# Small gate rows turned by plain transposes and added by VectorE, with the gathers of the next experts moved into the large blocks

## The chip, the core and the metric

The kernel runs on one core of one Trainium2 chip. The metric is device time in microseconds (us) of one execution.

## The reference: what is computed

One sequence of 256 tokens (two tiles of 128), model width 1024, float32. Layer 0 is retention and a dense SwiGLU; layer 1 is attention and a mixture of 8 experts, of which each token uses two. A layer norm follows each of the four parts. The change touches only the experts:

```
def swiglu(x, w_in, w_out):
    gate, up = jnp.split(x @ w_in, 2, axis=-1)
    return (jax.nn.silu(gate) * up) @ w_out

def moe_swiglu(x, router, w_in, w_out):
    ...
    for e in range(N_EXPERTS):
        out = out + gates[:, e:e + 1].astype(x.dtype) * swiglu(xt, w_in[e], w_out[e])
```

Each expert has a hidden width of 3584, so its weights are 1024 x 7168 and 3584 x 1024.

## The kernel before, in words

**Weights in units.** All weights stream through SBUF in units of 1 MB (128 x 2048 floats). SyncE issues one transfer for each unit into a ring of eight raw buffers (raw, more_raw). ScalarE copies the unit to its rounded high part (whi, whi_more), VectorE subtracts to get the low part (wlo, wlo_more), and TensorE multiplies with both. In the expert stage there are four such pairs, so ScalarE may split unit n + 4 only when TensorE is done with unit n (semaphore unit_used), and SyncE may refill a raw buffer only when VectorE is done with it (lo_done).

**Jobs.** The eight experts are sorted by how many tokens they have. They are worked in four pairs of a large job (up to 128 tokens) and a small job (up to 64 tokens); jobs 0, 2, 4, 6 are large and 1, 3, 5, 7 small. In a large job every weight unit takes 12 matmuls of 512 columns: x_hi with whi, x_hi with wlo, x_lo with whi. In a small job the 64 high and the 64 low token rows lie side by side in one 128-row operand, so that a unit takes 8 matmuls (with whi and with wlo). Rows 0 to 63 of the product then hold the part of the high rows, rows 64 to 127 that of the low rows, and the two have to be added.

**Blocks.** The hidden width of an expert is cut into blocks 0 to 3, of 1024, 1024, 1024 and 512 columns. A block has four gate units and four up units (two and two in block 3), and its output units follow a block later. The table STREAM lists all 336 units in the order of work: block b of the large job (gate units, output units of the block before, up units), then block b of the small job, then block b + 1 of the large job, and so on. Here such a piece of 8, 10 or 12 units is called a large stretch or a small stretch. START is the number of the first unit of a stretch, END that of the last unit of one part.

**Order on the engines.** Every engine runs the same loop over the unit number n, in its own queue. Tables such as GATE_TURN_AT say at which n it also does a piece of the work between. TensorE at n: unit n, then turns, then gathers. ScalarE at n: row copies, the high part of unit n + 4, then the small drains, then the copies of a gather. VectorE at n: the drains, then the low part of unit n + 4. So what VectorE does at n stands ahead of the low part of unit n + 4.

**The gate of a small block.** At END of the gate units ScalarE copies the two banks of gate rows to rows4. Two units later TensorE turns them by matmuls against the table merge (two identities of 64 one above the other, so that the product is transposed and the low row is added to the high row at once): turn_merged, 8 chunks (4 in block 3) into bank 0. Then ScalarE takes the silu into act_small. The up rows go the same way, and VectorE multiplies the two.

**Gathers.** The token rows of the next pair of jobs are gathered by matmuls with a selection matrix in 8 steps of 4 matmuls of 192 columns (gather_step), into bank 1; ScalarE copies each out (L956, L957). Before, three steps are in block 1 of the large job, three in block 1 of the small job and two in block 2 of the large job, for each of three pairs.

Of the kernel before, what the change touches and what calls it, by code (L numbers as in the profile page):

```python
# [6 lines left out]
ALU = mybir.AluOpType  # L7
# [7 lines left out]
P = 128  # L15
# [14 lines left out]
def build(nc, x, ln_g, ln_b, ret_w_in, ret_gn_g, ret_gn_b, ret_w_out, kv_w, moba_w_q, moba_w_out,  # L30
# [29 lines left out]
    JOBS = EX  # L60
# [26 lines left out]
    for phase in range(JOBS * (LAST + 1)):  # L87
# [5 lines left out]
        else:  # L93
# [12 lines left out]
    GATE_AT = {END[j, "gate", b]: (j, b) for j, b in SMALL_BLOCKS}  # L106
    GATE_TURN_AT = {END[j, "gate", b] + 2: (j, b) for j, b in SMALL_BLOCKS}
    UP_AT = {END[j, "up", b]: (j, b) for j, b in SMALL_BLOCKS}
    UP_TURN_AT = {END[j, "up", b] + 1: (j, b) for j, b in SMALL_BLOCKS}
# [4 lines left out]
                 for k, (j, b, i) in enumerate([(2 * pair - 2, 1, 5), (2 * pair - 2, 1, 7), (2 * pair - 2, 1, 9),  # L114
                                                (2 * pair - 1, 1, 5), (2 * pair - 1, 1, 7), (2 * pair - 1, 1, 9),
                                                (2 * pair - 2, 2, 5), (2 * pair - 2, 2, 7)])}
    SEL_AT = {START[j - j % 2, 2] + 1 + 3 * (j % 2): j for j in range(JOBS)}
# [29 lines left out]
    with ctx:  # L147
        def sem(name):
            return ctx.enter_context(nc.semaphore(name))
# [210 lines left out]
        gate_copied = sem("gate_copied")  # L360
        gate_turned = sem("gate_turned")
        small_silu = sem("small_silu")
        up_copied = sem("up_copied")
# [111 lines left out]
        def turn_bank(j, b, half):  # L475

            if j == 0 and b == 0:
                return 4 + half
            return 3 if b == LAST else 2 + half

        def sel_of(j):
# [184 lines left out]
        def _(act):  # L666
# [256 lines left out]
            def small_drains(n):  # L923

                if n in GATE_TURN_AT:
                    j, b = GATE_TURN_AT[n]
                    w = BLOCK_UNITS[b] * P
                    act.wait_ge(gate_turned, blocks(j, b))
                    if blocks(j, b) > 1:
                        act.wait_ge(small_lo, blocks(j, b) - 1)  # L930
                    nc.scalar.activation(act_small[:, 0:w], ps[:, 0, 0:w], ACT.Silu).then_inc(small_silu, 1)
                if n in SMALL_HI_AT:
# [89 lines left out]
        def _(dve):  # L1022
# [391 lines left out]
            def small_drains(n):  # L1414

                if n in SMALL_LO_AT:
                    j, b = SMALL_LO_AT[n]
                    c = 2 * BLOCK_UNITS[b]
                    gT = gT_small_of(j, b)
                    dve.wait_ge(small_hi, blocks(j, b))  # L1420
                    lo_of(gT[:, 0:c, HALF:P], act_small[:, 0:c * HALF].rearrange("p (c n) -> p c n", c=c),
                          gT[:, 0:c, 0:HALF]).then_inc(small_lo, 1)
                if n in SMALL_MUL_AT:
                    j, b = SMALL_MUL_AT[n]
# [76 lines left out]
        def _(pe):  # L1501
# [351 lines left out]
            def gather_pair(n):  # L1853

                pair, k = GATHER_AT[n]
                j, b = 2 * pair - 1 - (k in (0, 1, 2, 6, 7)), 2 if k >= 6 else 1
                if SMALL[j]:
                    pe.wait_ge(gate_copied, halves(j, b))
                else:
                    pe.wait_ge(big_silu, halves(j, b))  # L1860
                if k == 0:
# [48 lines left out]
            def big_unit(n):  # L1910

                j, part, b, q = STREAM[n]
                if q == 0 and part == "gate":
                    if b == 0 and j > 0:
                        pe.wait_ge(big_copied, KD * (j // 2))
                    if blocks(j, b) > 1:
                        pe.wait_ge(small_silu, blocks(j, b) - 1)
                        pe.wait_ge(gate_copied, 7 * (j // 2) + 2 * b)
# [65 lines left out]
            def small_turn(n):  # L1984

                if n in GATE_TURN_AT:
                    j, b = GATE_TURN_AT[n]
                    pe.wait_ge(gate_copied, halves(j, b))
                    turn_merged(rows4, 0, 2 * BLOCK_UNITS[b]).then_inc(gate_turned, 1)
                if n in UP_TURN_AT:  # L1990
# [102 lines left out]
```

## Time and profile before

| | us |
|---|---|
| median of 3 runs | 1430.73 (1428.29 to 1431.02) |
| the profiled execution: its own time | 1427.71 |
| the profiled execution: span of the core's instructions | 1426.0 |
| TensorE, VectorE, ScalarE busy in it | 1392.5, 1132.3, 959.8 |

The profile is that of one execution. Its rows are told in the section after the next. In the names of the rows PE is TensorE, PEld its weight loads, DVE VectorE, ACT ScalarE, SPq the queue of SyncE. A busy TensorE does not mean that it sets the time: its matmuls overlap, and a row's duration is longer than the distance to the next.

### The profile page before, as it was taken

How to read it: one execution, taken by the hardware profiler on the slowest of the kernel's cores; microseconds unless marked ns; L12 is line 12 of the kernel's file. 1: busy time of each engine (PE TensorE's matmuls, PEld its weight loads, DVE VectorE, ACT ScalarE, POOL GpSimd, SP SyncE). 2: the span in 40 equal slices, each digit the busy share in tenths (PEclk: the TensorE clock that was granted, in tenths of full speed). 3: DMA queues.
4: the chain of work that ended last, by engine and by line, in shares of the span. 5: the costliest groups of instructions: out<-in, count | busy, mean ns of one | idle time of the engine just before them, and what ended most of it. 6: DMA issues, size and time to landing. Idle time of an engine off the chain costs nothing.

```text
span 1426.0 us, 18557 instructions
## 1 busy us (share of the span) xinstructions
PE 1392.5 (98%) x7394; PEld 1182.6 (83%) x7394; DVE 1132.3 (79%) x791; ACT 959.8 (67%) x798; POOL 55.2 (4%) x64
## 2 busy tenths in 40 slices
PE   9999999999999999999999999999999999999995
PEld 9987789999979888888788788788788788787784
DVE  4456655454465678998999998999988999999996
ACT  5334544433454458797888797888787887787874
POOL 1002200000000003002000002000000000000000
PEclk9999999999999999999999999999999999999998
DMA  9654546555554329999999999999999999999990
GB/s 358 233 172 151 199 157 213 198 178 178 195 188 155 141 89 387 420 395 405 400 419 420 385 378 418 386 418 420 394 372 419 390 417 420 392 399 421 416 406 32
DMA packets 158743, 446.89 MB, mean 313 GB/s; under 512 B 7088, under 2 KB 46000, under 8 KB 158656
## 3 DMA queue, kind: packets, MB, share of 16 engines
q1 hardware_dynamic: 156832, 439.38, 80.5%
q0 software_dynamic: 1824, 6.33, 1.3%
q8 instruction: 57, 0.93, 0.2%
q14 instruction: 30, 0.25, 0.0%
HBM read 444.63 MB, written 1.05 MB: 313 GB/s over the span
## 4 chain that ended last, share of the span: by engine, by line
PE 68%; DVE 25%; issue 3%; ACT 3%; POOL 0%; DVEq 0%; ACTq 0%; POOLq 0%
PE ps L1504 20%; PE ps L1506 20%; PE ps L1505 20%; DVE wlo L1032 13%; DVE wlo_more L1032 6%; ACT whi L876 2%; PE ps L1980 2%; DVE gT_lo L1032 1%; DVE act L1400 1%; PE ps L1841 1%; DVE h L1391 1%; PE ps L1942 1%; PE ps L1943 1%; PE ps L1550 1%; DVE wlo L418 1%
## 5 line engine op out<-in xcount | busy, mean ns | idle before, releaser
L1032 DVE TENSOR_TENSOR wlo<-raw,whi 128x2048 fp32r<-128x2048 f32 (+1 forms) x214 | 479.1, 2259 | 33.5 <-ACT whi L876 32.8
L876 ACT ACTIVATE whi<-raw 128x2048 fp32r<-128x2048 f32 x208 | 395.7, 1918 | 107.4 <-PE ps L1506 100.7
L418 DVE TENSOR_TENSOR wlo<-raw,whi 128x2048 fp32r<-128x2048 f32 x80 | 183.6, 2294 | 155.3 <-ACT whi L411 155.3
L411 ACT ACTIVATE whi<-raw 128x2048 fp32r<-128x2048 f32 x82 | 156.8, 1912 | 153.2 <-PE ps L1506 149.7
L1504 PE MATMUL ps<-xT_hi,whi 128*128 128x256 f32 x576 | 163.3, 284 | 0.0
L1506 PE MATMUL ps<-xT_hi,wlo 128*128 128x256 f32 x576 | 163.0, 283 | 0.0
L1505 PE MATMUL ps<-xT_lo,whi 128*128 128x256 f32 x576 | 163.0, 283 | 0.0
L1504 PE MATMUL ps<-whi,xg_big 128*128 128x512 f32 x336 | 135.1, 402 | 3.4 <-DVE wlo L1032 3.4
L1942 PE MATMUL ps<-whi,xg_small 128*128 128x512 f32 x336 | 135.0, 402 | 2.7 <-DVE wlo L1032 1.8
L1506 PE MATMUL ps<-whi,xg_big 128*128 128x512 f32 x336 | 132.0, 393 | 0.0
L1505 PE MATMUL ps<-wlo,xg_big 128*128 128x512 f32 x336 | 131.5, 391 | 0.0
L1943 PE MATMUL ps<-wlo,xg_small 128*128 128x512 f32 x336 | 131.4, 391 | 0.0
L1504 PEld LDWEIGHTS ps<-xT_hi,whi 128*128 128x128 f32 x576 | 110.5, 192 | 0.5
L1505 PEld LDWEIGHTS ps<-xT_lo,whi 128*128 128x128 f32 x576 | 110.5, 192 | 0.4
L1506 PEld LDWEIGHTS ps<-xT_hi,wlo 128*128 128x128 f32 x576 | 110.5, 192 | 0.0
L1032 DVE TENSOR_TENSOR wlo<-more_raw,whi 128x2048 fp32r<-128x2048 f32 x42 | 96.1, 2288 | 9.3 <-ACT whi L876 9.3
L1032 DVE TENSOR_TENSOR wlo_more<-more_raw,whi_more 128x2048 fp32r<-128x2048 f32 x42 | 96.1, 2287 | 4.8 <-ACT whi_more L876 4.8
L1032 DVE TENSOR_TENSOR wlo_more<-raw,whi_more 128x2048 fp32r<-128x2048 f32 x42 | 96.1, 2287 | 3.8 <-ACT whi_more L876 3.8
L876 ACT ACTIVATE whi<-more_raw 128x2048 fp32r<-128x2048 f32 x42 | 80.6, 1918 | 18.8 <-PE ps L1506 13.6
L876 ACT ACTIVATE whi_more<-raw 128x2048 fp32r<-128x2048 f32 x42 | 80.6, 1920 | 12.3 <-PE ps L1506 12.3
L876 ACT ACTIVATE whi_more<-more_raw 128x2048 fp32r<-128x2048 f32 x42 | 80.7, 1920 | 12.2 <-PE ps L1506 12.2
L1504 PE MATMUL ps<-whi,xT_hi 128*128 128x512 f32 (+1 forms) x224 | 85.3, 381 | 2.4 <-DVE wlo L418 2.2
(269 smaller groups left out, 2686.5 us busy)
## 6 DMA issues: line engine op xcount, KB each, us to landing
raw<-in_moe_w_in SPq DMA_DIRECT2D x168, 1024.0 KB, 8.6
raw<-in_moe_w_out SPq DMA_DIRECT2D x84, 1024.0 KB, 7.8
more_raw<-in_moe_w_in SPq DMA_DIRECT2D x56, 1024.0 KB, 8.4
more_raw<-in_moe_w_out SPq DMA_DIRECT2D x28, 1024.0 KB, 8.2
raw<-in_ret_w_in SPq DMA_DIRECT2D x23, 1024.0 KB, 7.1
raw<-in_ffn_w_in SPq DMA_DIRECT2D x22, 1024.0 KB, 4.9
raw<-in_ffn_w_out SPq DMA_DIRECT2D x11, 1024.0 KB, 4.9
raw<-in_ret_w_out SPq DMA_DIRECT2D x8, 1024.0 KB, 4.9
```

Source lines behind the costliest of these rows:

```text
L411: nc.scalar.activation(whi[:, u % SPLIT, :], src, ACT.Copy).then_inc(hi_done, 1)
L418: nc.vector.tensor_tensor(wlo[:, u % SPLIT, :], src, whi[:, u % SPLIT, :].bitcast(F32), ALU.subtract).then_inc(lo_done, 1)
L876: nc.scalar.activation(moe_split(n)[0], moe_raw(n), ACT.Copy).then_inc(hi_done, 1)
L1032: return nc.vector.tensor_tensor(dst, src, hi.bitcast(F32), ALU.subtract)
L1391: nc.vector.scalar_tensor_tensor(out=h[:, t, :], in0=ps[:, at:at + 2, :].rearrange("p b n -> p (b n)"), scalar=gate, in1=h[:, t, :], op0=A ...
L1400: nc.vector.tensor_tensor(act4[:, cols], act4[:, cols], ps[:, 2 + half, :], ALU.mult).then_inc(big_mul, 1)
L1504: pe.matmul(dst, a_hi, b_hi, start=start, stop=False, skip_group_check=True)
L1505: pe.matmul(dst, a_hi, b_lo, start=False, stop=False, skip_group_check=True)
L1506: return pe.matmul(dst, a_lo, b_hi, start=False, stop=stop, skip_group_check=True)
L1942: pe.matmul(dst, a, hi, start=start, stop=False, skip_group_check=True)
L1943: return pe.matmul(dst, a, lo, start=False, stop=stop, skip_group_check=True)
L1980: last = pe.matmul(ps[:, at, c * HALF:(c + 1) * HALF], rows[:, c * P:(c + 1) * P], merge[:, :], start=True, stop=True)
```

## The change

Five things are done. The gate rows of a small block are turned by plain transposes against the identity, each of which writes 128 columns, so that the result takes two banks (0 and 1) and the low part is not yet added (turned_gate names the two halves). ScalarE copies the low half to act_small where it took the silu before. VectorE adds the high half at END of gate + 3 (GATE_SUM_AT). ScalarE takes the silu in place at END of gate + 6, or + 4 in the very last small block (SMALL_SILU_AT). And all gathers stand in large blocks: three in block 1, three in block 2 and two in block 3 of the large job. The up rows are still turned against merge.

```diff
--- before.py
+++ after.py
@@ -105,6 +105,8 @@
     LO_AT = {END[j, "up", b] + 3 + half: (j, b, half) for j, b, half in BIG_HALVES}
     GATE_AT = {END[j, "gate", b]: (j, b) for j, b in SMALL_BLOCKS}
     GATE_TURN_AT = {END[j, "gate", b] + 2: (j, b) for j, b in SMALL_BLOCKS}
+    GATE_SUM_AT = {END[j, "gate", b] + 3: (j, b) for j, b in SMALL_BLOCKS}
+    SMALL_SILU_AT = {END[j, "gate", b] + (4 if (j, b) == (JOBS - 1, LAST) else 6): (j, b) for j, b in SMALL_BLOCKS}
     UP_AT = {END[j, "up", b]: (j, b) for j, b in SMALL_BLOCKS}
     UP_TURN_AT = {END[j, "up", b] + 1: (j, b) for j, b in SMALL_BLOCKS}
     SMALL_MUL_AT = {END[j, "up", b] + 2: (j, b) for j, b in SMALL_BLOCKS}
@@ -112,8 +114,8 @@
     SMALL_LO_AT = {END[j, "up", b] + 5: (j, b) for j, b in SMALL_BLOCKS}
     GATHER_AT = {START[j, b] + i: (pair, k) for pair in range(1, JOBS // 2)
                  for k, (j, b, i) in enumerate([(2 * pair - 2, 1, 5), (2 * pair - 2, 1, 7), (2 * pair - 2, 1, 9),
-                                                (2 * pair - 1, 1, 5), (2 * pair - 1, 1, 7), (2 * pair - 1, 1, 9),
-                                                (2 * pair - 2, 2, 5), (2 * pair - 2, 2, 7)])}
+                                                (2 * pair - 2, 2, 5), (2 * pair - 2, 2, 7), (2 * pair - 2, 2, 9),
+                                                (2 * pair - 2, 3, 3), (2 * pair - 2, 3, 5)])}
     SEL_AT = {START[j - j % 2, 2] + 1 + 3 * (j % 2): j for j in range(JOBS)}
     Y_AT = {END[j, "out", LAST]: j for j in range(JOBS - 1)}
     SCATTER_AT = {END[j, "out", LAST] + (4 + 4 * t if j < JOBS - 2 else 3 + 3 * t): (j, t) for j in range(JOBS - 1) for t in range(T)}
@@ -359,6 +361,8 @@
         big_lo = sem("big_lo")
         gate_copied = sem("gate_copied")
         gate_turned = sem("gate_turned")
+        gate_half = sem("gate_half")
+        gate_summed = sem("gate_summed")
         small_silu = sem("small_silu")
         up_copied = sem("up_copied")
         up_turned = sem("up_turned")
@@ -477,6 +481,9 @@
             if j == 0 and b == 0:
                 return 4 + half
             return 3 if b == LAST else 2 + half
+
+        def turned_gate():
+            return ps[:, 0:2, :].rearrange("p a (c s n) -> p (a c) s n", s=2, n=HALF)
 
         def sel_of(j):
             return sel[:, j // 2 % 2, :, j % 2 * P:(j % 2 + 1) * P]
@@ -924,11 +931,17 @@
 
                 if n in GATE_TURN_AT:
                     j, b = GATE_TURN_AT[n]
-                    w = BLOCK_UNITS[b] * P
+                    c = 2 * BLOCK_UNITS[b]
                     act.wait_ge(gate_turned, blocks(j, b))
                     if blocks(j, b) > 1:
                         act.wait_ge(small_lo, blocks(j, b) - 1)
-                    nc.scalar.activation(act_small[:, 0:w], ps[:, 0, 0:w], ACT.Silu).then_inc(small_silu, 1)
+                    nc.scalar.activation(act_small[:, 0:c * HALF].rearrange("p (c n) -> p c n", c=c),
+                                         turned_gate()[:, 0:c, 1, :], ACT.Copy).then_inc(gate_half, 1)
+                if n in SMALL_SILU_AT:
+                    j, b = SMALL_SILU_AT[n]
+                    w = BLOCK_UNITS[b] * P
+                    act.wait_ge(gate_summed, blocks(j, b))
+                    nc.scalar.activation(act_small[:, 0:w], act_small[:, 0:w], ACT.Silu).then_inc(small_silu, 1)
                 if n in SMALL_HI_AT:
                     j, b = SMALL_HI_AT[n]
                     c = 2 * BLOCK_UNITS[b]
@@ -1420,6 +1433,12 @@
                     dve.wait_ge(small_hi, blocks(j, b))
                     lo_of(gT[:, 0:c, HALF:P], act_small[:, 0:c * HALF].rearrange("p (c n) -> p c n", c=c),
                           gT[:, 0:c, 0:HALF]).then_inc(small_lo, 1)
+                if n in GATE_SUM_AT:
+                    j, b = GATE_SUM_AT[n]
+                    c = 2 * BLOCK_UNITS[b]
+                    rows = act_small[:, 0:c * HALF].rearrange("p (c n) -> p c n", c=c)
+                    dve.wait_ge(gate_half, blocks(j, b))
+                    nc.vector.tensor_tensor(rows, rows, turned_gate()[:, 0:c, 0, :], ALU.add).then_inc(gate_summed, 1)
                 if n in SMALL_MUL_AT:
                     j, b = SMALL_MUL_AT[n]
                     w = BLOCK_UNITS[b] * P
@@ -1853,11 +1872,7 @@
             def gather_pair(n):
 
                 pair, k = GATHER_AT[n]
-                j, b = 2 * pair - 1 - (k in (0, 1, 2, 6, 7)), 2 if k >= 6 else 1
-                if SMALL[j]:
-                    pe.wait_ge(gate_copied, halves(j, b))
-                else:
-                    pe.wait_ge(big_silu, halves(j, b))
+                pe.wait_ge(big_silu, halves(2 * pair - 2, 1 + k // 3))
                 if k == 0:
                     pe.wait_ge(sel_ready, 2 * T * pair)
                 pe.wait_ge(small_copied, gathers(pair) + k)
@@ -1914,7 +1929,7 @@
                     if b == 0 and j > 0:
                         pe.wait_ge(big_copied, KD * (j // 2))
                     if blocks(j, b) > 1:
-                        pe.wait_ge(small_silu, blocks(j, b) - 1)
+                        pe.wait_ge(gate_summed, blocks(j, b) - 1)
                         pe.wait_ge(gate_copied, 7 * (j // 2) + 2 * b)
                     if gathered_by(START[j, b]):
                         pe.wait_ge(small_copied, gathered_by(START[j, b]))
@@ -1986,7 +2001,9 @@
                 if n in GATE_TURN_AT:
                     j, b = GATE_TURN_AT[n]
                     pe.wait_ge(gate_copied, halves(j, b))
-                    turn_merged(rows4, 0, 2 * BLOCK_UNITS[b]).then_inc(gate_turned, 1)
+                    for c in range(2 * BLOCK_UNITS[b]):
+                        last = pe.transpose(ps[:, c // 4, c % 4 * P:(c % 4 + 1) * P], rows4[:, c * P:(c + 1) * P], ident[:, :])
+                    last.then_inc(gate_turned, 1)
                 if n in UP_TURN_AT:
                     j, b = UP_TURN_AT[n]
                     pe.wait_ge(up_copied, halves(j, b))
```

The lists below are the order of instructions on an engine, before and after. A line number of after.py is not that of before.py: L1032 became L1045 (the low part), L1428 became L1447 (multiply by up), L876 became L883 (the high part), L1841 became L1860 (gather).

**VectorE, small stretch of block 1 of job 3, before**, from the second drain of the large job (gT_lo) to the end of the stretch's splits:

```order
L1032 TENSOR_TENSOR gT_lo<-ps,gT_hi 128x512 [waits big_hi]
L1032 TENSOR_TENSOR wlo_more<-more_raw,whi_more 128x2048 [waits hi_done]
L1032 TENSOR_TENSOR wlo<-raw,whi 128x2048 [waits hi_done] x3
L1032 TENSOR_TENSOR wlo_more<-raw,whi_more 128x2048 [waits hi_done]
L1032 TENSOR_TENSOR wlo<-raw,whi 128x2048 [waits hi_done] x2
```

The same place after:

```order
L1045 TENSOR_TENSOR gT_lo<-ps,gT_hi 128x512 [waits big_hi]
L1045 TENSOR_TENSOR wlo_more<-more_raw,whi_more 128x2048 [waits hi_done]
L1045 TENSOR_TENSOR wlo<-raw,whi 128x2048 [waits hi_done] x2
L1441 TENSOR_TENSOR act_small<-act_small,ps 128x512 [waits gate_half]
L1045 TENSOR_TENSOR wlo<-raw,whi 128x2048 [waits hi_done]
L1045 TENSOR_TENSOR wlo_more<-raw,whi_more 128x2048 [waits hi_done]
L1045 TENSOR_TENSOR wlo<-raw,whi 128x2048 [waits hi_done] x2
```

The sum (L1441) stands three splits ahead of the end; the first of the last two wlo rows is the first unit of the next large stretch, so the sum stands ahead of that.

**TensorE, large stretch of block 3 of job 0**, from the fourth unit (its output products, gT_hi) into the fifth, before:

```order
L1504 MATMUL ps<-whi_more,gT_hi 128x512
L1505 MATMUL ps<-wlo_more,gT_hi 128x512
L1506 MATMUL ps<-whi_more,gT_lo 128x512
L1504 MATMUL ps<-whi,gT_hi 128x512
L1505 MATMUL ps<-wlo,gT_hi 128x512
```

and after:

```order
L1524 MATMUL ps<-wlo_more,gT_hi 128x512
L1525 MATMUL ps<-whi_more,gT_lo 128x512
L1860 MATMUL ps<-sel,h_hi 128x192 x2
L1860 MATMUL ps<-sel,h_lo 128x192 x2
L1523 MATMUL ps<-whi,gT_hi 128x512
```

A gather step has come in between the two units. The same happens two units later, and once more in block 2.

**ScalarE, the very last small block (job 7, block 3)**, from its up rows (L907) on, before:

```order
L907 ACTIVATE rows_116<-ps 128x512
L876 ACTIVATE whi_more<-raw 128x2048
L931 ACTIVATE act_small<-ps 128x256
L876 ACTIVATE whi<-raw 128x2048 x2
L963 ACTIVATE y_hi_106<-ps 128x512 x2
L876 ACTIVATE whi<-more_raw 128x2048
```

and after:

```order
L914 ACTIVATE rows_116<-ps 128x512
L883 ACTIVATE whi_more<-raw 128x2048
L938 ACTIVATE act_small<-ps 128x256
L883 ACTIVATE whi<-raw 128x2048 x2
L944 ACTIVATE act_small<-act_small 128x256
L976 ACTIVATE y_hi_106<-ps 128x512 x2
L883 ACTIVATE whi<-more_raw 128x2048
```

The silu (L944) now stands behind the two splits that it stood ahead of (as L931), and VectorE's multiply in that block stands ahead of the low part of the second of these two units.

## Rows read from the trace of the kernel before

**Rows 1.** The page: busy time by engine; the chain that ended last, by engine.

```profile
PE 1392.5 (98%) x7394; PEld 1182.6 (83%) x7394; DVE 1132.3 (79%) x791; ACT 959.8 (67%) x798; POOL 55.2 (4%) x64
...
PE 68%; DVE 25%; issue 3%; ACT 3%; POOL 0%; DVEq 0%; ACTq 0%; POOLq 0%
```

**Rows 2.** Waits, 540 to 1402 us: who waited for whom, us, times, longest.

```profile
ACT whi L876 <- PE ps L1506: 113.6, 119, 3.5
...
PE ps L1504 <- DVE wlo L1032: 3.4, 14, 0.5
```

**Rows 3.** SyncE's own queue, 600 to 1400 us, the same columns.

```profile
SPq L544 <- DVE wlo L1032: 471.4, 225, 3.5
```

**Rows 4.** Chain in order of time, 820 to 960 us: start, us, what.

```profile
826.09 1.93 ACT whi L876
...
843.73 6.60 DVE wlo L1032 x3
...
852.54 2.21 DVE wlo L1032
854.88 0.47 PE ps L1504
...
857.89 1.73 PE ps L1980 x16
...
873.84 0.42 PE ps L1841 x4
...
955.31 2.22 DVE wlo L1032
957.66 0.47 PE ps L1504
```

**Rows 5.** The same view, 735 to 800 us.

```profile
791.58 0.47 PE ps L1504
```

**Rows 6.** Busy time by stretch: TensorE, weight loads, VectorE, ScalarE, GpSimd; clock, DMA share, GB/s.

```profile
828.00:854.80 26.80, 26.70 (x136) 22.10 (x134) 26.77 (x16) 25.72 (x25) 0.00 (x0) 1.00 1.01 380
854.90:890.00 35.10, 35.10 (x168) 29.37 (x169) 30.48 (x15) 26.08 (x23) 7.96 (x4) 1.00 1.02 418
```

**Rows 7.** VectorE's groups by shape, 540 to 1402 us: busy us, mean ns.

```profile
L1428 DVE TENSOR_TENSOR act_small<-act_small,ps 128x512 f32<-128x512 f32 x12 | 8.2, 682 | 0.0
L1428 DVE TENSOR_TENSOR act_small<-act_small,ps 128x256 f32<-128x256 f32 x4 | 1.7, 413 | 0.0
```

**Rows 8.** VectorE in order of time, from 830 us: start, us, what.

```profile
830.24 0.68 DVE L1400 TENSOR_TENSOR act<-act,ps 128x512 f32<-128x512 f32 x1
830.84 2.28 DVE L1032 TENSOR_TENSOR wlo_more<-raw,whi_more 128x2048 fp32r<-128x2048 f32 x1
```

**Rows 9.** ScalarE in order of time, 837 to 850 us.

```profile
843.38 0.61 ACT L931 ACTIVATE act_small<-ps 128x512 f32<-128x512 f32 x1
```

**Rows 10.** TensorE in order of time, from 612.4 us, and from 1411 us.

```profile
612.40 0.39 PE L1943 MATMUL ps<-wlo,xg_small 128*128 128x512 f32 x1
612.63 0.60 PE L1906 MATMUL ps<-ident,act 128*128 128x128 f32 x4
612.98 0.48 PE L1942 MATMUL ps<-whi,xg_small 128*128 128x512 f32 x1
...
1412.88 0.63 PE L1877 MATMUL ps<-y_lo_last,selT 128*128 128x512 f32 x1
1413.31 0.63 PE L1876 MATMUL ps<-y_hi_last,selT 128*128 128x512 f32 x1
```

**Rows 11.** VectorE, then ScalarE, in order of time, end of the expert stage.

```profile
1392.76 2.29 DVE L1032 TENSOR_TENSOR wlo<-raw,whi 128x2048 fp32r<-128x2048 f32 x1 [0.73 <-ACT whi L876]
1394.96 0.41 DVE L1428 TENSOR_TENSOR act_small<-act_small,ps 128x256 f32<-128x256 f32 x1
1396.42 2.30 DVE L1032 TENSOR_TENSOR wlo<-raw,whi 128x2048 fp32r<-128x2048 f32 x1 [1.04 <-ACT whi L876]
...
1394.47 1.92 ACT L876 ACTIVATE whi<-raw 128x2048 fp32r<-128x2048 f32 x1 [1.75 <-PE ps L1506]
```

## The prediction

> **What bounds the kernel now.** I read the page first. TensorE is busy for 98% of the span and VectorE for 79%, which would make TensorE the bound everywhere; but the chain that ended last gives TensorE 68% and VectorE 25% [rows 1]. A quarter of the time is therefore set by VectorE. The question is where.
>
> The chain in order of time answers it. At 826.09 it passes from TensorE to a split on ScalarE (whi), and from there to VectorE. From then until 854.88 it holds only VectorE pieces: three low parts in a row from 843.73, and the last one at 852.54, which is the first unit of the next large stretch. At 854.88 it goes back to TensorE, at the first matmul of that unit [rows 4]. The same handing over stands at 957.66, after the low part at 955.31 [rows 4], and at 791.58 [rows 5]. So a large stretch is set by TensorE (12 matmuls for each unit), and a small one (8 matmuls for each unit) by VectorE, whose low part costs 2.20 us of chain whatever the job. The stretches show it too: between 828.00 and 854.80 VectorE is busy for 26.77 of 26.80 us, and between 854.90 and 890.00 for only 30.48 of 35.10 [rows 6].
>
> The waits agree. TensorE's first matmul of a large unit (L1504) waits for VectorE's low part 14 times, 3.4 us in all [rows 2]: short, but it means that at the end of the small stretches TensorE had already caught up with VectorE. In the other direction ScalarE waits 119 times for TensorE (L1506, large units) [rows 2], which is how a large stretch holds back the splits. Do the transfers bind? SyncE's queue waits 471.4 us for VectorE to give a buffer back [rows 3], and no wait of an engine for a landing stands among the waits that I read. They do not.
>
> **The change, part by part.** The price of each edit hangs on whether it stands in a large stretch (TensorE sets the end) or in a small one (VectorE does).
>
> *Fewer passes on TensorE.* A merge matmul runs as two passes: 8 chunks are x16 in the chain and take 1.73 us [rows 4], 0.108 a pass. Four plain transposes start at 612.63 and the next matmul at 612.98; that one takes 0.48 us where its like take 0.39, so four cost some 0.43, or 0.108 each [rows 10]. A chunk so falls from 0.216 to 0.108 us. There are 12 wide small blocks of 8 chunks and 4 narrow ones of 4, 112 chunks in all: TensorE is given 12.1 us less to do. All of it lies in small stretches, under VectorE's work, and there TensorE is the one that waits. I take it as nothing. Its bounds are 0 and -12.1.
>
> *The sum on VectorE.* It is a tensor_tensor from act_small and PSUM, the form of L1428: 0.682 us for 512 columns, 0.413 for 256 [rows 7]. Consecutive instructions overlap: one of 0.68 us starts at 830.24 and the next at 830.84 [rows 8], so in a full queue a wide sum costs 0.60 and, with the same overlap of 0.08, a narrow one 0.33. It stands ahead of the low part of unit END of gate + 7. In blocks 1 and 2 this is two units ahead of the next large stretch, in blocks 0 and 3 the first unit of that stretch. Either way it is ahead of the low part for which TensorE waits. Two blocks differ. In job 1, block 0, where no output units stand between gate and up, the sum comes behind the low part of the large stretch's second unit, and the large stretch covers it. In job 7, block 3, it falls into a gap of 0.73 us ahead of 1392.76 [rows 11]. That leaves 11 wide and 3 narrow ones on the path: 11 x 0.60 + 3 x 0.33 = 7.6 us.
>
> Does VectorE also wait there? The sum needs ScalarE's copy, and that stands where the silu stood: 843.38, for 0.61 us [rows 9]. The sum's place is between the second and the third of the low parts that run from 843.73 [rows 4], at 848.1. ScalarE is over 4 us early, so I take no wait. The copy of the low half reads as many columns as the silu did, so I price it the same. The sum reads PSUM in runs of 64 columns, which no VectorE row here shows; from below I price it at the 0.60 above, from above at double, 7.6 us more.
>
> *The silu on its own.* ScalarE gets one more activation for each small block, at most 0.61 us [rows 9]. ScalarE is busy for 25.72 of the 26.80 us of a small stretch [rows 6], which is close, but three pairs of gather copies leave that stretch, and the silu comes four units after the old one, when VectorE's multiply is still four units away. I take it as nothing, except at the end.
>
> *The end.* In job 7, block 3, the silu stands behind the high part of unit 333, which starts at 1394.47 and takes 1.92 us; VectorE's multiply stands ahead of the low part of unit 333. Now that multiply runs at 1394.96, in a gap, and the low part starts at 1396.42 as soon as the high part is there [rows 11]. After the change the order is high part (to 1396.4), silu (0.3), multiply (0.33), low part: it starts at about 1397.1, 0.7 us late. From there VectorE's work is in one piece into the last output units. +0.7 us; at worst +1.0.
>
> *The gathers.* A step of four matmuls takes 0.42 us of chain [rows 4]. Three for each of three pairs leave a small stretch, where TensorE gains nothing by it, and enter large stretches, where TensorE sets the time: +1 in block 2 and +2 in block 3. I looked at whether they still stand ahead of the place where the chain leaves TensorE. In block 2 that is ten units in, and the last gather follows the unit before; in block 3 it is six units in, and the gathers follow units three and five. So 9 x 0.42 = 3.8 us; the lower bound is 0, if VectorE had lain ahead there. The ScalarE copies go into the 2.7 us (12 x 0.23 [rows 10]) for each unit of a large stretch, where ScalarE is busy for 26.08 of 35.10 us [rows 6].
>
> *Waits.* TensorE's next gate units now wait for the sum (gate_summed) and no longer for the silu. Behind that wait stand the matmuls of the whole large stretch; but they wait for a later low part of the same queue anyway, so it is never the last to come.
>
> Sum: 7.6 + 0.7 + 3.8 = +12.1 us. The profiled execution's own time is 1427.71, of which 1426.0 is the span: that gives 1439.8 and 1438.1. The median before is 3.0 us above that execution, so against it the same change gives 1442.8; I say 1442.5.
>
> **The rivals.**
>
> *Faster: the saving on TensorE counts.* If TensorE set the small stretches too, the change would take away up to 12.1 us there and the sums would be covered. With the gathers only moved from one bound place to another, the time would be about 1419. For it: 98% busy. Against it: the chain and the 14 waits. It decides at the handing over: where TensorE reaches the large stretch's first unit later than its low part, the saving counts, and there only until the 0.60 us sum has used it up. 4%.
>
> *No change: the transfers set the pace.* The DMA share is 1.01 in the small stretch [rows 6], so a memory-bound stage would hide the sums, the gathers and the saving alike: 1431. The chain has no transfer in it, and SyncE waits for VectorE, not VectorE for a landing. 3%. The Trainium skill (Perfetto Trace Analysis, Roofline) says that a single core can be taken to have its ceiling at about 120% of 358 GB/s, bounded by 16 DMA engines of some 435 GB/s together; by that rule the 418 GB/s of a large stretch is nearly full and no VectorE term would count. The waits in this trace speak against it.
>
> *Dearer sums.* The short PSUM runs or a wait make each sum cost up to double, or the sums shift a second thing late: 1447 to 1451. 7%.
>
> *Cheaper.* The gathers or some of the sums find cover: 1434 to 1438. 7%.
>
> *The clock.* TensorE waits longer at the end of each small stretch (some 2 to 3 us more, what it saves plus the sum), right behind a burst of transposes. If the granted clock fell there to the lower level, the matmuls would be 0.43 us apart, as at the end of this trace (1412.88 to 1413.31) [rows 10], in place of 0.23 (612.40 to 612.63): a large unit would take 2.4 us longer, and one such unit in each of 14 stretches 34 us, or 1477. Against it: a clock of 1.00 in both stretches, with four transposes twice in each small one [rows 6]. 2%. The Trainium skill (TensorE: Matmul & The Clock Gate, Part 4: PE-mode transpose) says that transposes do not count as busy for the clock, and 8 in a row would by it be a risk that merge was not.
>
> **How the numbers follow.** My forecast, 1439.5 to 1446 by itself, has 77%. The range takes in the cheaper case from 1437 and the dearer one to 1449. A measurement here tells 0.2% (2.9 us) from no change; everything from 1434 up is slower. So slower 0.92, within 0.2% 0.04, faster 0.04.
>
> **What would show it.** Right: L1441 x16 on VectorE at about 0.68 and 0.41 us and in the chain 14 times; the small stretches of blocks 1 to 3 longer by one sum; waits of TensorE for VectorE's low part up from a few us to 25 or so, since TensorE arrives early; gathers in the chain nine times more; transposes x112 where 224 merge passes were. Wrong: a chain without L1441, VectorE idle ahead of it, or a clock under 1.00 in a small stretch.

## The result and the profile after

| | before | after |
|---|---|---|
| median (range) | 1430.34 us (1428.29 to 1431.02), 4 runs | 1446.57 us (1446.14 to 1450.81), 4 runs |
| ratio, 95% interval | | 1.0125 (1.011 to 1.014) |
| profiled execution, its span | 1427.71, 1426.0 us | 1446.54, 1444.8 us |

The change makes the kernel 1.25% slower. The medians are 16.2 us apart, the two profiled spans 18.8 us. Lines have moved: the low part is now L1045, the high part L883, a large unit's matmuls L1523 to L1525, a small unit's L1957 and L1958, the merge L1995, a gather step L1860, VectorE's multiply L1447. New are L1441 (the sum), L944 (the silu by itself) and L2005 (the plain turns).

The page after: busy time, then the share of each engine in the chain that ended last.

```profile
PE 1391.5 (96%) x7282; PEld 1171.3 (81%) x7282; DVE 1141.0 (79%) x807; ACT 967.2 (67%) x814; POOL 54.9 (4%) x64
PE 66%; DVE 27%; issue 4%; ACT 3%; POOL 0%; DVEq 0%; ACTq 0%; POOLq 0%
```

Against [rows 1] the span has grown by 18.8 us and TensorE's busy time has not: it gained idle time. Between 600 and 1400 us it was idle for 7.8 us before (busy 792.19 of 800) and is idle for 22.2 us after (busy 777.77). VectorE has 16 instructions more, and a larger share of the chain. Where TensorE's idle time is, the waits after between 540 and 1421 say (total us, times, longest):

```profile
PEld ps L1957 <- DVE wlo L1045: 18.7, 22, 1.7
PEld ps L1957 <- DVE wlo_more L1045: 15.5, 23, 0.9
PE ps L1957 <- DVE wlo L1045: 10.7, 19, 1.3
PE ps L1523 <- DVE wlo L1045: 6.1, 14, 1.1
DVE act_small L1447 <- ACT act_small L944: 4.5, 2, 2.8
PEld ps L1523 <- DVE act_small L1441: 3.3, 1, 3.3
```

The first two are waits of the weight loads of a small stretch for the low parts, with their matmuls' own waits in the third; in the same view of before the first two were this:

```profile
PEld ps L1942 <- DVE wlo L1032: 7.8, 13, 1.0
PEld ps L1942 <- DVE wlo_more L1032: 5.7, 15, 0.5
```

The handing over to a large stretch (fourth row) is still there 14 times, and has grown from 3.4 us [rows 2] to 6.1. TensorE works faster through a small stretch and then waits longer for VectorE. The last row is new and was not forecast: one single wait of 3.3 us for the sum.

The chain after, around the same stretches as [rows 4]:

```profile
852.17 2.20 DVE wlo_more L1045
854.37 4.41 DVE wlo L1045 x2
858.78 0.60 DVE act_small L1441
859.37 2.20 DVE wlo L1045
...
866.13 0.47 PE ps L1523
...
869.13 1.73 PE ps L1995 x16
...
885.12 0.42 PE ps L1860 x4
...
891.01 0.42 PE ps L1860 x4
...
896.91 0.42 PE ps L1860 x4
```

The sum stands in the chain for 0.60 us, between two low parts with no gap, and the three gathers of block 2 stand in the part where the chain is on TensorE. Between 560 and 1421 the chain has 15 such pieces of L1441: 12 of 0.59 to 0.61 and 3 of 0.33 us. A gather step stands in it 24 times (21 of 0.42 and 3 of 0.52 us), against 15 before (12 and 3): nine more, as forecast. VectorE's groups by form and TensorE's turns (busy us, mean ns):

```profile
L1441 DVE TENSOR_TENSOR act_small<-act_small,ps 128x512 f32<-128x512 f32 x12 | 8.2, 683 | 0.0
L1441 DVE TENSOR_TENSOR act_small<-act_small,ps 128x256 f32<-128x256 f32 x4 | 1.7, 415 | 0.0
```

```profile
L2005 PE MATMUL ps<-ident,rows 128*128 128x128 f32 x112 | 14.8, 272 | 0.0
```

The sum costs what the multiply costs [rows 7], although it reads PSUM in runs of 64 columns.

**Where the 18.8 us lie.** Stages can be cut where VectorE starts the low part of a given unit. Unit 0 is the first of the experts, unit 16 the first of the large stretch that follows the first small one, unit 28 the first of the next small stretch, unit 324 the first of the last small stretch. Two of these marks in the timeline of VectorE, of before and then of after (start, duration, instruction):

```profile
602.59 2.29 DVE L1032 TENSOR_TENSOR wlo<-raw,whi 128x2048 fp32r<-128x2048 f32 x1 [0.89 <-ACT whi L876]
1372.11 2.29 DVE L1032 TENSOR_TENSOR wlo<-raw,whi 128x2048 fp32r<-128x2048 f32 x1
```

```profile
609.76 2.29 DVE L1045 TENSOR_TENSOR wlo<-raw,whi 128x2048 fp32r<-128x2048 f32 x1 [0.88 <-ACT whi L883]
1390.67 2.28 DVE L1045 TENSOR_TENSOR wlo<-raw,whi 128x2048 fp32r<-128x2048 f32 x1
```

All kernels of this study, cut the same way (the rows above are units 28 and 324):

| kernel | start of unit 0 | 0 to 16 | 16 to 28 | 28 to 324 | 324 to end |
|---|---|---|---|---|---|
| before | 524.1 | 46.4 | 32.1 | 769.5 | 53.8 |
| after | 526.9 | 46.4 | 36.4 | 780.9 | 54.1 |
| e1_first_sum_early | 527.1 | 50.8 | 32.6 | 780.9 | 53.6 |
| e2_gathers_only | 524.0 | 46.4 | 32.1 | 773.4 | 53.0 |
| e3_vector_op_only | 524.0 | 46.4 | 32.1 | 777.1 | 52.9 |
| e4_turns_no_sum | 527.3 | 46.4 | 32.1 | 773.5 | 52.9 |
| e7_wait_only | 524.0 | 46.4 | 36.4 | 769.4 | 52.9 |
| e6_gathers_small | 526.8 | 46.4 | 32.1 | 766.4 | 53.0 |
| e5_up_rows_instead | 527.1 | 50.7 | 31.2 | 758.4 | 53.1 |
| e8_up_rows_gathers_small | 524.9 | 46.4 | 31.1 | 755.7 | 52.2 |

Each row is one execution. Where nothing was edited and the clock is alike, the stages agree within 0.1 us: 46.4, 32.1, and 769.5 in before with 769.4 in e7.

So 18.8 = 2.8 ahead of the experts + 4.3 in the first large stretch after a small one + 11.4 in the long middle + 0.3 at the end. The 2.8 us are not counted as the change's: no edit touches that code, and the granted clock between 200 and 300 is 0.98 in this execution and 1.00 in that of before. e6, which is made from the kernel before, has them too (526.8). e4, made from the changed kernel, has them in its profiled execution (1434.07 us), and others of its runs took 3.4 us less (1430.71). The two parts to explain are the 11.4 and the 4.3; the 0.3 at the end hides a term of the change and is taken up with the prediction.

### The profile page after: what moved, and what is told of

It is laid out like the page before. It is cut to its first block, busy times and chain, and to the rows that moved or that the text cites. A ratio compares the mean times of both kernels' runs of the same rounds, so it can differ in the third digit from the quotient of the medians.

```text
span 1444.8 us, 18365 instructions
## 1 busy us (share of the span) xinstructions
PE 1391.5 (96%) x7282; PEld 1171.3 (81%) x7282; DVE 1141.0 (79%) x807; ACT 967.2 (67%) x814; POOL 54.9 (4%) x64
## 4 chain that ended last, share of the span: by engine, by line
PE 66%; DVE 27%; issue 4%; ACT 3%; POOL 0%; DVEq 0%; ACTq 0%; POOLq 0%
PE ps L1523 20%; PE ps L1525 20%; PE ps L1524 20%; DVE wlo L1045 14%; DVE wlo_more L1045 6%; ACT whi L883 2%; PE ps L1995 2%; PE ps L1860 1%; DVE gT_lo L1045 1%; DVE act L1413 1%; DVE h L1404 1%; DVE wlo L422 1%; PE ps L1569 1%; DVE act_small L1441 1%; DVE h L1088 1%
## 5 line engine op out<-in xcount | busy, mean ns | idle before, releaser
L1045 DVE TENSOR_TENSOR wlo<-raw,whi 128x2048 fp32r<-128x2048 f32 (+1 forms) x214 | 479.8, 2261 | 36.5 <-ACT whi L883 35.9
L883 ACT ACTIVATE whi<-raw 128x2048 fp32r<-128x2048 f32 x208 | 396.1, 1920 | 113.6 <-PE ps L1525 105.8
L1523 PE MATMUL ps<-xT_hi,whi 128*128 128x256 f32 x576 | 163.7, 284 | 0.0
L1525 PE MATMUL ps<-xT_hi,wlo 128*128 128x256 f32 x576 | 163.3, 284 | 0.0
L1957 PE MATMUL ps<-whi,xg_small 128*128 128x512 f32 x336 | 136.5, 406 | 11.0 <-DVE wlo L1045 10.7
L1523 PE MATMUL ps<-whi,xg_big 128*128 128x512 f32 x336 | 136.3, 406 | 8.9 <-DVE wlo L1045 6.1
L1525 PE MATMUL ps<-whi,xg_big 128*128 128x512 f32 x336 | 132.4, 394 | 0.0
L1958 PE MATMUL ps<-wlo,xg_small 128*128 128x512 f32 x336 | 131.7, 392 | 0.0
L1523 PEld LDWEIGHTS ps<-xT_hi,whi 128*128 128x128 f32 x576 | 110.7, 192 | 0.5
L1525 PEld LDWEIGHTS ps<-xT_hi,wlo 128*128 128x128 f32 x576 | 110.6, 192 | 0.0
L1045 DVE TENSOR_TENSOR wlo<-more_raw,whi 128x2048 fp32r<-128x2048 f32 x42 | 96.1, 2289 | 9.8 <-ACT whi L883 9.8
L1045 DVE TENSOR_TENSOR wlo_more<-more_raw,whi_more 128x2048 fp32r<-128x2048 f32 x42 | 96.1, 2288 | 4.4 <-ACT whi_more L883 4.4
L1045 DVE TENSOR_TENSOR wlo_more<-raw,whi_more 128x2048 fp32r<-128x2048 f32 x42 | 96.1, 2288 | 3.8 <-ACT whi_more L883 3.8
L883 ACT ACTIVATE whi<-more_raw 128x2048 fp32r<-128x2048 f32 x42 | 80.7, 1920 | 18.2 <-PE ps L1525 12.9
L1957 PEld LDWEIGHTS ps<-whi,xg_small 128*128 128x128 f32 x336 | 63.1, 188 | 36.1 <-DVE wlo L1045 18.7
L883 ACT ACTIVATE whi_more<-raw 128x2048 fp32r<-128x2048 f32 x42 | 80.7, 1922 | 13.3 <-PE ps L1525 12.5
L883 ACT ACTIVATE whi_more<-more_raw 128x2048 fp32r<-128x2048 f32 x42 | 80.7, 1921 | 13.1 <-PE ps L1525 12.2
```

The source lines that it names most:

```text
L883: nc.scalar.activation(moe_split(n)[0], moe_raw(n), ACT.Copy).then_inc(hi_done, 1)
L1045: return nc.vector.tensor_tensor(dst, src, hi.bitcast(F32), ALU.subtract)
L1523: pe.matmul(dst, a_hi, b_hi, start=start, stop=False, skip_group_check=True)
L1525: return pe.matmul(dst, a_lo, b_hi, start=False, stop=stop, skip_group_check=True)
L1957: pe.matmul(dst, a, hi, start=start, stop=False, skip_group_check=True)
L1958: return pe.matmul(dst, a, lo, start=False, stop=stop, skip_group_check=True)
```

## The experiments

Eight kernels, in two sessions. Each session ran the kernel before as well: 1428.84 us in the first (e1 to e4), 1429.14 in the second. Every ratio is to the kernel before of the same session. Theory A is that of the prediction: VectorE's sums and TensorE's gathers are added, TensorE's saving is not. The rest was open: the 4.3 us. Of each edit the lines that matter are shown; ... marks a cut inside a piece, and lines that go with them (new semaphores, the wait ahead of a gather step) are left out.

### e1_first_sum_early: the first sum one unit earlier

After, with this:

```
-    GATE_SUM_AT = {END[j, "gate", b] + 3: (j, b) for j, b in SMALL_BLOCKS}
+    GATE_SUM_AT = {END[j, "gate", b] + (2 if (j, b) == (1, 0) else 3): (j, b) for j, b in SMALL_BLOCKS}
```

> The changed kernel, with the one sum of job 1, block 0, placed one unit earlier in VectorE's queue, ahead of the low part of unit 17. Theory (a wait that I left out): TensorE waits at unit 16 for that sum, 2.89 us, and the clock falls behind it; so the wait shrinks to about 0.5 us, the clock stays at 1.00 there, and the time is about 4 us below the changed kernel's 1446.6, near 1442.5, that is 12 above before. Rival (the 4 us came with the run, not with the wait): the time stays within 1.5 us of 1446.6 and the clock dips at the same place.

Measured: 1442.28 us (1439.46 to 1446.82), ratio to before 1.0079 (1.0055 to 1.0103). The stretch 16 to 28 falls from 36.4 to 32.6 us. The wait between 560 and 640, and the window 560 to 580 (busy us of PE, PEld, DVE, ACT, POOL, then the granted clock):

```profile
PEld ps L1523 <- DVE act_small L1441: 1.1, 1, 1.1
```

```profile
560.00:580.00 20.00, 19.48 (x94) 15.71 (x92) 17.66 (x11) 18.80 (x14) 0.00 (x0) 1.00 1.03 421
```

The wait falls from 3.3 to 1.1 us, the clock stays at 1.00, and 3.8 of the 4.3 us are gone. The other 0.5 us is the sum's own, which the chain of e1 still holds (580.24, 0.61 us): the first matmul of unit 16 starts 2.94 us after the start of that unit's low part (580.89 and 577.95), against 2.43 in the kernel before (572.92 and 570.49). The span of the profiled execution, 1445.1, does not show the gain, since in it the clock was 0.83 between 520 and 560, where 0 to 16 took 50.8 us in place of 46.4. That is ahead of the place of the edit, and e5 shows the same. The medians agree in sign and are less exact: 13.4 us over before in e1, 16.2 after the change.

### e2_gathers_only: before, with the gathers moved

```
-                                                (2 * pair - 1, 1, 5), (2 * pair - 1, 1, 7), (2 * pair - 1, 1, 9),
-                                                (2 * pair - 2, 2, 5), (2 * pair - 2, 2, 7)])}
+                                                (2 * pair - 2, 2, 5), (2 * pair - 2, 2, 7), (2 * pair - 2, 2, 9),
+                                                (2 * pair - 2, 3, 3), (2 * pair - 2, 3, 5)])}
```

> The kernel before, with only the gathers moved into the large blocks. Theory (large stretches are set by TensorE, small ones by VectorE): 9 steps of 0.42 us enter the path and nothing leaves it, +3.8 us. Rival (the small stretches are set by TensorE too, or the gathers are covered in the large ones): within 1 us of before.

Measured: 1433.52 us (1430.53 to 1439.03), ratio 1.0035 (1.0017 to 1.0052). The middle grows from 769.5 to 773.4, by 3.9 us; the forecast term was 3.8.

### e3_vector_op_only: before, with one more VectorE instruction

Before, and VectorE takes the maximum of act_small with itself (the same value) in 15 small blocks, where the sum stands after the change; the merge stays.

```
+                if n in GATE_SUM_AT:
+                    ...
+                    nc.vector.tensor_tensor(act_small[:, 0:w], act_small[:, 0:w], act_small[:, 0:w],
+                                            ALU.max).then_inc(gate_summed, 1)
```

> The kernel before, with one more VectorE operation in every small block but the first, at the place of the sum: the maximum of act_small with itself (512 or 256 columns, the result unchanged). Theory: VectorE sets the small stretches, so 11 wide ones at 0.60 and 3 narrow ones at 0.33 us cost 7.6 us. Rival (TensorE or the transfers set them): under 1 us. If the sum of the changed kernel is dearer than this for its way of reading PSUM, this run shows less per operation than the changed kernel does.

Measured: 1435.56 us (1434.31 to 1446.14), ratio 1.0057 (1.0037 to 1.0077). The middle is 777.1 us, 7.6 more than before: 11 wide at 0.60 and 3 narrow at 0.33.

### e4_turns_no_sum: after, without the sum

The silu reads the turned high rows straight from PSUM; the low part of the small gate rows is left out of the result, so that nothing is added on VectorE. The separate silu and the sum are gone, and TensorE waits for the silu again in place of the sum. The gathers and the plain transposes are as after.

```
-                                         turned_gate()[:, 0:c, 1, :], ACT.Copy).then_inc(gate_half, 1)
+                                         turned_gate()[:, 0:c, 0, :], ACT.Silu).then_inc(small_silu, 1)
```

> The changed kernel without the sum: the silu is taken straight from the high half, where the copy was, and the low part of the small gate rows is left out. It has the plain transposes and the moved gathers. Theory: the 12 us that TensorE is given less to do are worth nothing, so it costs what the gathers alone cost, +3.8 us over before. Rival (the saving on TensorE counts): up to 12 us below that, some 8 us faster than before.

Measured: 1432.25 us (1430.71 to 1442.05), ratio 1.0024 (1.0005 to 1.0044). The middle is 773.5 us, the same as e2's 773.4: 112 plain transposes in place of 224 merge passes are worth nothing there. What TensorE is given back turns into waiting, as the waits between 600 and 1400 show; both groups are larger than those of before:

```profile
PEld ps L1946 <- DVE wlo_more L1040: 14.5, 22, 0.9
PEld ps L1946 <- DVE wlo L1040: 13.8, 22, 1.7
```

### e7_wait_only: before, with the first block's wait alone

e3's instruction in job 1, block 0 only, and TensorE waits for it where it waits for the sum of that block after the change:

```
+                        pe.wait_ge(gate_summed, 1)
```

> The kernel before, with one VectorE operation more, in job 1, block 0 alone, at the place where the changed kernel has its sum, and with TensorE's next gate units waiting for it. Theory (a wait that I left out): TensorE waits for it at unit 16, about 2.9 us, the clock falls for a few us behind that wait, and the first large stretch grows by about 4.3 us; all else as before, so +4. Rival (the rest of the change brought those 4 us): no more than 0.6 us.

Measured: 1433.7 us (1430.93 to 1442.67), ratio 1.0031 (1.0013 to 1.0048). The stretch 16 to 28 takes 36.4 us, exactly as after; the other stages are those of before, or of e2 and e3 where these did not touch them. TensorE's timeline, of before at the first matmul of unit 16 and then of e7:

```profile
572.92 0.47 PE L1504 MATMUL ps<-whi,xg_big 128*128 128x512 f32 x1
```

```profile
572.42 0.39 PE L1953 MATMUL ps<-wlo_more,xg_small 128*128 128x512 f32 x1
575.60 0.51 PE L1513 MATMUL ps<-whi,xg_big 128*128 128x512 f32 x1 [2.79 <-DVE act_small L1429]
575.90 0.63 PE L1514 MATMUL ps<-wlo,xg_big 128*128 128x512 f32 x1
576.33 0.63 PE L1515 MATMUL ps<-whi,xg_big 128*128 128x512 f32 x1
...
579.32 0.40 PE L1513 MATMUL ps<-whi,xg_big 128*128 128x512 f32 x1
579.55 0.39 PE L1514 MATMUL ps<-wlo,xg_big 128*128 128x512 f32 x1
```

One wait for one short instruction, without a transpose or a gather moved, gives the whole 4.3 us. Unit 16 starts 2.7 us later than before (575.60 against 572.92; unit 0 starts at 524.0 and 524.1). The other 1.6 us come behind the start, where the matmuls are 0.43 us apart (575.90, 576.33) up to 579.32, where they are 0.23 apart again: 3.7 us hold some nine of them, 0.20 us further apart each, which by this estimate makes 1.7 us.

### e6_gathers_small: the gathers the other way

Before, with the two steps per pair that stood in block 2 of the large job put into block 2 of the small job.

```
-                                                (2 * pair - 2, 2, 5), (2 * pair - 2, 2, 7)])}
+                                                (2 * pair - 1, 2, 5), (2 * pair - 1, 2, 7)])}
```

> The kernel before, with the two gather steps of each pair that stood in block 2 of the large job moved to block 2 of the small job: the opposite of the change. Theory: TensorE waits there for VectorE about 0.85 us in each stretch, room for two steps of 0.42, and 6 steps leave the large stretches: up to 2.5 us faster. Rival (no room, the steps cost the same there): no change.

Measured: 1425.81 us (1423.46 to 1431.98), ratio 0.9973 (0.9956 to 0.9989). The middle falls by 3.1 us; the chain has 9 gather steps in place of 15, and six of 0.42 are 2.5. Where the other 0.6 us comes from was not traced.

### e5_up_rows_instead: the same trade in the other kind of stretch

Gate rows as before; now it is the up rows (in all small blocks but the last) that are turned plainly and added by VectorE. They are turned one unit after the end of the up units, that is inside the next large stretch, where TensorE sets the time and VectorE has gaps.

```
+                if n in UP_TURN_AT and UP_TURN_AT[n] in UP_SUM:
+                    ...
+                    nc.scalar.activation(up_small[:, 0:c * HALF].rearrange("p (c n) -> p c n", c=c),
+                                         turned_up()[:, 0:c, 1, :], ACT.Copy).then_inc(up_half, 1)
...
+                        nc.vector.tensor_tensor(rows, rows, turned_up()[:, 0:c, 0, :], ALU.add).then_inc(up_summed, 1)
```

The two turns of the selection matrix move to four and six units into block 2, since they share a bank.

> The kernel before, with the gate rows as they were and the up rows of the small blocks (but the very last) turned by plain transposes, the low half copied by ScalarE, added by VectorE and then multiplied. These turns stand in the first unit of a large stretch. Theory (in a large stretch TensorE sets the time and VectorE has room): TensorE's saving now counts, 12 wide blocks at 0.86 and 3 narrow ones at 0.43 us, 11.6 us faster, and the sums cost nothing. Rival (VectorE's sums cost wherever they stand, since it has only just emptied its queue there): the 7.6 us of the sums come off that, 4 us faster or no change.

Measured: 1417.59 us (1414.67 to 1422.21), ratio 0.9903 (0.9883 to 0.9923). The middle falls by 11.1 us. The chain, and VectorE's timeline at the same place:

```profile
855.72 2.21 DVE wlo L1045
858.07 0.47 PE ps L1527
...
861.04 0.87 PE ps L2018 x8
```

```profile
866.65 0.68 DVE L1443 TENSOR_TENSOR rows<-rows,ps 128x512 f32<-128x512 f32 x1
867.36 0.69 DVE L1446 TENSOR_TENSOR act_small<-act_small,rows 128x512 f32<-128x512 f32 x1
...
877.86 2.29 DVE L1045 TENSOR_TENSOR wlo<-raw,whi 128x2048 fp32r<-128x2048 f32 x1 [0.39 <-ACT whi L883]
```

The turn is in the chain, at 0.87 in place of 1.73 us [rows 4]; the sum is not, for the chain has gone over to TensorE at 858.07, and VectorE is waiting again at 877.86.

### e8_up_rows_gathers_small: e5 and e6 together

> Both of the last two together. Theory: the gains add up, 14 us faster than before. Rival: as for each.

Measured: 1412.24 us (1411.37 to 1418.75), ratio 0.9881 (0.9859 to 0.9904): 17 us better than before, and 33 better than after when each is taken against the kernel before of its own session; it is the fastest of this study. The middle is 13.8 us shorter than before's, close to 11.1 + 3.1.

## Why the prediction was right

The forecast was 1442.5 us, in a range of 1437 to 1449, slower; it is 1446.57. Sign, mechanism and the sizes of the main terms hold; one step failed and cost 4 us. With these 4 us the time lies 0.6 us above the band that the forecast gave itself, 1439.5 to 1446, and inside the range only by the part that was added for dearer sums. The sums were not dearer. That the range held is so in part luck: the room left for one error took in another.

- **What bounds the kernel.** Right. The same 0.60 us instruction costs its full price at the end of the small stretches (e3) and nothing in the large one (e5). Passes saved on TensorE are worth nothing in the small (e4) and count in full in the large one (e5): the middle has 100 of its chunks, 100 x 0.108 = 10.8 us, and got 11.1 us shorter; 16 to 28 has 8, 0.9 us, and went from 32.1 to 31.2.
- **Fewer passes on TensorE.** Right: 773.5 with them and 773.4 without.
- **The sum on VectorE.** Right: 7.6 forecast and 7.6 measured (e3), at 0.60 and 0.33 us of chain. The short PSUM runs cost nothing (683 ns, [rows 7] has 682). The sum of job 1, block 0, which the large stretch was to cover, comes in the chain too, so that L1441 is there 15 times and not 14; of its own it costs 0.5 us (e1).
- **The gathers.** Right: 3.8 forecast, 3.9 measured (e2). With the sums that makes the 11.4 of the middle.
- **The silu on its own.** Right. In job 1, block 0 VectorE's multiply waited for it, 2.78 us, and in e1 1.4 us. The large stretch hid that: e1's stretch takes 0.5 us more than before's, and TensorE's later start at unit 16, which is the sum's, accounts for all of it.
- **The end.** Right: 0.7 forecast, 0.6 measured. In the tail the orders are as forecast, high part, silu, multiply, low part. ScalarE's timeline, then VectorE's:

```profile
1413.03 1.92 ACT L883 ACTIVATE whi<-raw 128x2048 fp32r<-128x2048 f32 x1 [1.75 <-PE ps L1525]
1414.85 0.40 ACT L944 ACTIVATE act_small<-act_small 128x256 f32<-128x256 f32 x1
```

```profile
1410.50 0.42 DVE L1441 TENSOR_TENSOR act_small<-act_small,ps 128x256 f32<-128x256 f32 x1
...
1415.28 0.42 DVE L1447 TENSOR_TENSOR act_small<-act_small,ps 128x256 f32<-128x256 f32 x1 [1.67 <-ACT act_small L944]
1415.62 2.29 DVE L1045 TENSOR_TENSOR wlo<-raw,whi 128x2048 fp32r<-128x2048 f32 x1
```

The high part ends at 1413.03 + 1.92 = 1414.95 and the low part starts at 1415.62, 0.67 us later, against 0.03 before (1394.47 + 1.92 to 1396.42, [rows 11]). Counted from the mark of unit 324, that low part starts 24.95 us after the change (1390.67 to 1415.62) and 24.31 before (1372.11 to 1396.42), 0.64 us later. The whole last stage says the same only where the clock is alike: e1, which has the changed end, took 53.6 us against 52.9 to 53.0 in e2, e3, e4 and e7. In the profiled executions of before (53.8) and after (54.1) the clock fell earlier: it is 0.86 between 1405 and 1415 in before and 0.89 between 1424 and 1434 in after, against 1.00 in e2 (1408 to 1418) and in e7 (1409 to 1419). No edit explains that.

- **Waits: the step that failed.** The prediction said of the units behind that wait: "they wait for a later low part of the same queue anyway, so it is never the last to come". That is so where output units stand between gate and up. In job 1, block 0 there are none. The prediction had seen that, and used it only to say that the sum lies behind other work and is covered; its price for this wait was nothing. But the gate units that end this block are 8 to 11, so the sum stands at loop 14, behind the low part of unit 17, and TensorE's next gate unit, which now waits for it, is unit 16. TensorE has the low part that it needs and still waits for a low part that it does not need yet, and for the sum behind it. After the change, VectorE's timeline and then TensorE's:

```profile
573.38 4.49 DVE L1045 TENSOR_TENSOR wlo<-raw,whi 128x2048 fp32r<-128x2048 f32 x2
577.78 0.69 DVE L1441 TENSOR_TENSOR act_small<-act_small,ps 128x512 f32<-128x512 f32 x1
```

```profile
575.24 0.39 PE L1958 MATMUL ps<-wlo_more,xg_small 128*128 128x512 f32 x1
578.52 0.80 PE L1523 MATMUL ps<-whi,xg_big 128*128 128x512 f32 x1 [2.89 <-DVE act_small L1441]
579.12 0.63 PE L1524 MATMUL ps<-wlo,xg_big 128*128 128x512 f32 x1
579.54 0.63 PE L1525 MATMUL ps<-whi,xg_big 128*128 128x512 f32 x1
```

The first of the two low parts is unit 16's and ends near 575.6; TensorE starts at 578.52. It then finds the lower clock: matmuls 0.42 us apart (579.12, 579.54), 1.2 GHz in place of 2.4. e7 makes the same 4.3 us out of the wait alone, e1 takes 3.8 of them away. So the price is shown to be the wait's, with the clock's fall that follows it: 2.7 us of later start and 1.6 us at the lower clock (e7).

- **The clock rival.** It had 2%, for a fall in every handing over behind the transposes. It did not come in that form: the clock is 1.00 between 600 and 1400, with 100 of the 112 transposes and 14 waits at a handing over in it.

```profile
600.00:1400.00 800.00, 777.77 (x3592) 627.64 (x3592) 752.73 (x428) 655.59 (x513) 16.78 (x10) 1.00 1.01 398
```

The Trainium skill (TensorE: Matmul & The Clock Gate, Part 4: PE-mode transpose) says that transposes do not count as busy for the clock. Whether that is so no run here tells; bursts of 8 between matmuls left the clock at 1.00. What did fall was the clock once in the first large stretch after a small one, behind a wait, and in e7 it fell in the same way with no plain transpose in the small rows.

- **No change, because of the transfers.** Excluded: e8 streams the same weights in 1412.24 us.

Sum by the stages: 7.6 + 3.9 + 4.3 + 0.6 = 16.4 us, beside 16.2 between the medians.

## What to carry to other kernels

Before a piece of work is handed from one engine to another, ask for each stage which engine ends last there: the same trade was worth +7.6 us in the small stretches and -11.1 us in the large ones. When a new wait is said to be covered by a later wait on the same queue, check it for the irregular first block too: count, unit by unit, what stands in the queue ahead of the signal and what the waiting engine really needs at that moment. Work that can float (the gathers here) belongs where its engine waits anyway.

## What the runs showed of the hardware

- One wait of TensorE's matmuls of 2.8 to 2.9 us in the timeline (2.79 in e7, 2.89 after; 3.3 for the weight load after) was followed by the lower clock: in e7 from 575.60 to about 579.3, with matmuls 0.43 us apart and then 0.23. The waits in the small stretches brought no such fall: after, the longest between 600 and 1400 is 1.3 us for a matmul and 1.7 for a weight load, and the clock there is 1.00. Nor did e1's wait of 0.7 us for the matmul and 1.1 for the load. Where between these the fall begins was not tried.

The windows of after around it (the last three numbers: granted clock, DMA share, GB/s):

```profile
570.00:575.00 5.00, 4.49 (x24) 3.49 (x23) 5.00 (x4) 5.00 (x4) 0.00 (x0) 1.00 1.03 421
575.00:580.00 5.00, 2.11 (x7) 1.38 (x6) 5.00 (x4) 3.42 (x4) 0.00 (x0) 0.85 1.03 422
580.00:585.00 5.00, 5.00 (x28) 4.37 (x27) 2.87 (x2) 1.81 (x1) 0.00 (x0) 0.81 1.02 418
585.00:590.00 5.00, 5.00 (x24) 4.11 (x23) 2.29 (x1) 2.36 (x3) 0.00 (x0) 1.00 1.03 421
```

- Ahead of the experts the same code took 524.0 to 527.3 us in ten profiled executions, with the granted clock between 200 and 300 at 1.00 or below it (0.98 after), and from unit 0 to unit 16 it took 46.4 us, but 50.7 or 50.8 in e1 and e5 (clock 0.83 between 520 and 560 in e1). What decides that from one execution to the next was not found. It is as large as some of the terms measured here, which is why the stages were compared and not the spans.
- A merge matmul of 64 columns in float32 and a plain transpose of 128 columns differ by a factor of two for a chunk: 1.73 us of chain for 8 merged chunks, 0.87 for 8 transposed ones (e5).
